# Hybrid diffusion block on one core: paired value products in the array's columns, norms by tile, latent norms inside the window attention, modulation rows turned by transposes, twelve expert slots in layer 1

## The reference

```python
mod = silu(c) @ ada_w + ada_b                       # 6 x 1024, for latent and for context
h = modulate(rms_norm(x, norm1), mod[0], mod[1])
z = h @ w_in                                        # one projection, 15 parts
oa = neighbourhood_attention(...)                   # 4 heads of 64, keys: window + 256 context
q, k, v = mla_heads(rms_norm(dq), rms_norm(dkv), kr)   # latent norms, rotary part
ob = block_attention(q, k, v)                       # 4 heads, 96-wide scores, 64-wide values
oc = gated_linear_attention(...)                    # two directions, chunks of 64
y = (sigmoid(m_a)*(oa @ w_br_a) + sigmoid(m_b)*(ob @ w_br_b) + sigmoid(m_c)*(oc @ w_br_c)) @ w_out
x = x + mod[2] * y
x = x + mod[5] * expert_choice_moe(modulate(rms_norm(x, norm2), mod[3], mod[4]))   # 16 experts, 1024 x 1024 x 3
```

## Time and profile before

| | us |
|---|---|
| median of 3 runs | 2928.09 |
| the profiled execution's own time | 2929.94 |
| its span | 2928.2 |
| TensorE busy (matmul) | 2626.2 |
| VectorE busy | 1042.5 |
| ScalarE busy | 689.8 |
| GpSimd busy | 73.1 |

### The profile page before, as it was taken

One profiled execution on the slowest core, in us unless ns is written; L12 is line 12 of the kernel. 1 busy time (PEld: TensorE's weight loads), 2 busy tenths in 40 slices (PEclk: granted clock), 3 DMA queues, 4 the chain that ended last, 5 costly groups with the idle time before them and its releaser, 6 DMA issues.

```text
span 2928.2 us, 42639 instructions
## 1 busy us (share of the span) xinstructions
PE 2626.2 (90%) x17806; PEld 1726.6 (59%) x17806; DVE 1042.5 (36%) x2187; ACT 689.8 (24%) x1330; POOL 73.1 (2%) x131
## 2 busy tenths in 40 slices
PE   5999999899997699999999689999899768999996
PEld 3888877677775535453454478787677642433332
DVE  3534344333672412212221563444347421111112
ACT  2521122322441212121121262133235210110101
POOL 1000100000000000000000000000000000000000
PEclk7999999999998699999999799999899879999998
DMA  5110465155532088786979211132115329999995
GB/s 196 51 44 30 122 195 173 51 166 168 201 136 115 11 329 349 290 347 259 378 283 364 97 36 59 44 101 69 62 51 180 152 91 409 382 407 378 410 386 232
DMA packets 239139, 571.27 MB, mean 195 GB/s; under 512 B 11079, under 2 KB 119857, under 8 KB 237937
## 3 DMA queue, kind: packets, MB, share of 16 engines
q1 hardware_dynamic: 231200, 547.07, 50.4%
q0 software_dynamic: 7760, 21.60, 2.4%
HBM read 548.64 MB, written 19.98 MB: 194 GB/s over the span
## 4 chain that ended last, share of the span: by engine, by line
PE 82%; DVE 8%; DMA 5%; ACT 3%; issue 2%; SPq 0%; DVEq 0%; POOL 0%; ACTq 0%
PE ps L890 12%; PE ps L1305 11%; PE ps L917 11%; PE ps L1435 6%; PE ps L1256 4%; PE ps L1239 4%; PE ps L1149 3%; DMA arena<-in_moe_w_up 3%; PE ps L1454 3%; PE ps L1477 2%; PE ps L1498 2%; PE ps L1328 2%; PE ps L1332 2%; PE ps L859 2%; PE ps L1388 1%
## 5 line engine op out<-in xcount | busy, mean ns | idle before, releaser
L1305 PE MATMUL ps<-arena 128*32 128x512 f32 x2304 | 344.1, 605 | 5.9 <-issue 4.9
L917 PE MATMUL ps<-h_hi,m_lo 128*128 128x512 f32 (+1 forms) x1152 | 345.9, 371 | 1.7 <-DVE arena L1997 1.7
L1306 PE MATMUL ps<-arena 128*32 128x512 f32 x768 | 343.7, 605 | 0.0
L1435 PE MATMUL ps<-arena 128*64 128x512 f32 x1024 | 238.9, 613 | 30.8 <-DMA arena<-in_moe_w_up 27.5
L890 PE MATMUL ps<-m_lo,h_hi 128*128 128x256 f32 (+1 forms) x1248 | 238.6, 293 | 5.5 <-DVE m_lo L1970 3.9
L917 PEld LDWEIGHTS ps<-h_hi,m_lo 128*128 128x128 f32 x1152 | 207.8, 190 | 53.6 <-issue 16.8
L1305 PEld LDWEIGHTS ps<-arena 128*32 128x32 f32 x2304 | 93.7, 112 | 229.4 <-issue 226.8
L890 PEld LDWEIGHTS ps<-m_lo,h_hi 128*128 128x128 f32 x1248 | 198.0, 196 | 17.1 <-issue 12.5
L917 PE MATMUL ps<-h_lo,m_lo 128*128 128x512 f32 (+1 forms) x576 | 204.9, 356 | 0.0
L1435 PEld LDWEIGHTS ps<-arena 128*64 128x64 f32 x1024 | 74.6, 140 | 181.9 <-issue 178.0
L890 PE MATMUL ps<-m_lo,h_lo 128*128 128x256 f32 (+1 forms) x624 | 178.2, 286 | 0.0
(11 more groups left out here) (360 smaller groups left out, 4408.4 us busy)
## 6 DMA issues: line engine op xcount, KB each, us to landing
arena<-in_moe_w_gate SPq DMA_DIRECT2D x128, 1024.0 KB, 6.8
arena<-in_moe_w_up SPq DMA_DIRECT2D x128, 1024.0 KB, 8.5
arena<-in_moe_w_down SPq DMA_DIRECT2D x128, 1024.0 KB, 8.3
ring<-in_w_in SPq DMA_DIRECT2D x42, 1024.0 KB, 5.4
arena<-in_ada_w SPq DMA_DIRECT2D x40, 1024.0 KB, 5.5
mix_spill<-arena POOLq DMA_DIRECT2D x48, 256.0 KB, 2.8
ring<-in_w_out SPq DMA_DIRECT2D x4, 2048.0 KB, 10.2
arena<-in_ada_w SPq DMA_DIRECT2D x3, 2048.0 KB, 21.2
```

What stands on the lines that cost most here:

```text
L917: last = mm(to, w[:, k, cols], h[:, k, seg], start=n == 0 and k == 0, stop=n == 2 and k == KD - 1)
L1305: mm(ps[r][32 * b:32 * b + 32, :], c_xg[:, k, j, 32 * b:32 * b + 32], w, start=k == 0, stop=k == KD - 1)
L1306: last = mm(ps[r][96:128, :], c_xg[:, k, j, 32 * r:32 * r + 32], up[:, kk, 512:1024], start=k == 0, stop=k == KD - 1)
L1435: last = mm(bank[64 * c:64 * c + 64, :], p_xg[:, k, j, :], p_raw[(i + c) % PAIR_SLOTS][:, kk, 512 * half:512 * half + 512], start=k == 0, ...
```

## The change

1. **Values.** The two heads of a pair are done together, at every second iteration: v (128 x 64) is now the weight, the turned probabilities (128 x 128) the moving data, and the two heads write partitions 0 to 63 and 64 to 127 of the bank, interleaved. The result is already turned. The sums come as two more products, ones (128 x 64) with a diagonal of the inverted sums (`inverted`, VectorE), and VectorE multiplies the two. The transposes and copies after the attention are gone; the window attention's result waits in `na_oT` and GpSimd copies it to `oT` once. The latent attention's units now go pair by pair as well.
2. **Modulation rows** are turned by two transposes; VectorE adds the four groups in the copy.
3. **Norms by tile**: square, root, inversion and scaling of a tile stand behind that tile's last addition, with the next tiles' additions between. The second half of the gate rows is made between the output projection's tiles. The chunk and spill transfers at the start of layer 1 are issued tile by tile or earlier, and the small memsets of `scan_keep` and `rpb_pad` stand after the first jobs. The final result is stored by tile.
4. **Latent norms** stand inside the window attention: squares of tile u in unit u (0 to 5), root at 6, scaling of tile u-6 in units 6 to 11.
5. **Expert slots**: 12 in layer 1, the four new ones in `x_sb`, `oT` and free parts of the arena.

The core of the diff:

```diff
+SLOTS_OF = (PAIR_SLOTS, PAIR_SLOTS + 4)
...
-        o_tok = carve(ar, 90, NT, 256)
+        na_oT = carve(ar, 90, 2, TOK)
+        sum_diag = carve(ar, 70, 2, P)
...
-        diag, gated = carve(oTf, 0, 4, P), carve(ar, 24, SEQ)
+        diag, gated = carve(ar, 26, 4, P), carve(ar, 24, SEQ)
...
+        p_raw = [carve(ar, 8 * i, 2, D) for i in range(PAIR_SLOTS)] + [carve(x_flat, 0, 2, D), carve(oTf, 0, 2, D), carve(ar, 74, 2, D), carve(ar, 82, 2, D)]
...
+                    sp.wait_ge(hidT_up, before("hidT_up", l))
                     chunk_load(l, 0)
-                    sp.dma_start(x_spill.rearrange("(t p) d -> p t d", p=P), x_sb[:, CT:NT, :]).then_inc(x_saved, 16)
+                    for t in range(CT, NT):
+                        sp.wait_ge(x_ok, before("x_ok", l) - 2 * (NT - 1 - t))
+                        sp.dma_start(x_spill[(t - CT) * P:(t - CT + 1) * P, :], x_sb[:, t, :]).then_inc(x_saved, 16)
                     chunk_load(l, 1)
...
-                    sp.wait_ge(p_used, before("p_used", l) + g * PER_TURN + (i + 1))
+                    sp.wait_ge(p_used, before("p_used", l) + g * PER_TURN + (i + 1 - SLOTS_OF[l] + PAIR_SLOTS))
                     src = a["moe_w_" + matrix][l, bass.ds(g * GE + j, 1), kp * 256:kp * 256 + 256, :]
-                    sp.dma_start(p_raw[i % PAIR_SLOTS], src.rearrange("e (k p) n -> p (e k) n", p=P)
-                                 ).then_inc(pair_in[i % PAIR_SLOTS], 16)
+                    sp.dma_start(p_raw[i % SLOTS_OF[l]], src.rearrange("e (k p) n -> p (e k) n", p=P)
+                                 ).then_inc(pair_in[i % SLOTS_OF[l]], 16)
...
-            sp.wait_ge(fin_ok, SEQ // P)
-            sp.dma_start(out[0].rearrange("(t p) d -> p t d", p=P), fin).then_inc(stored, 16)
-            sp.wait_ge(stored, 16)
+            for ti in range(SEQ // P):
+                sp.wait_ge(fin_ok, ti + 1)
+                sp.dma_start(out[0][ti * P:(ti + 1) * P, :], fin[:, ti, :]).then_inc(stored, 16)
+            sp.wait_ge(stored, 16 * (SEQ // P))
...
+                    if 2 * i == sum(at[0] == "na" for at in MIX_AT[l]):
+                        pool.wait_ge(o_ok, before("o_ok", 2 * l + 1))
+                        cols = slice(q_tiles(l)[0] * P, TOK)
+                        nc.gpsimd.tensor_copy(oT[:, 0:2, cols], na_oT[:, :, cols]).then_inc(na_moved, 1)
...
-                            last = mm(ada_bank(h)[:, 256 + 2 * c:258 + 2 * c], ada_row[0:ADA_ROWS, tile(c)], col_sum[0:ADA_ROWS, :],
-                                      start=True, stop=True)
+                            last = tr(ada_bank(h)[:, 256 + P * c:256 + P * c + ADA_ROWS], ada_row[0:ADA_ROWS, tile(c)], ident[0:ADA_ROWS, 0:ADA_ROWS])
...
-                        pe.wait_ge(o_ok, before("o_ok", idx) + u)
+                    if u >= 2:
+                        pe.wait_ge(o_ok, before("o_ok", idx) + u // 2)
...
+                def values(p):
+                    t = us[2 * p][1]
                     if t >= CT:
-                        pe.wait_ge(p_act, before("p_act", idx) + lats[u])
-                    pe.wait_ge(p_dve, before("p_dve", idx) + u + 1)
+                        pe.wait_ge(p_act, before("p_act", idx) + lats[2 * p + 1])
+                    pe.wait_ge(p_dve, before("p_dve", idx) + 2 * p + 2)
                     keys = range(NT if t >= CT else CT)
                     for kt in keys:
-                        v = nav[:, kt, 64 * h:64 * h + 64] if i == 0 else mv[:, kt, h, :]
-                        last = mm(ps[5][:, 256:320], probT[:, u % 2, kt, :], v, start=kt == 0, stop=kt == keys[-1])
+                        for e in range(2):
+                            h = us[2 * p + e][0]
+                            v = nav[:, kt, 64 * h:64 * h + 64] if i == 0 else mv[:, kt, h, :]
+                            mm(ps[5][64 * e:64 * e + 64, 256:384], v, probT[:, e, kt, :], start=kt == 0, stop=kt == keys[-1])
+                    pe.wait_ge(sum_ok, before("sum_ok", idx) + 2 * p + 2)
+                    for e in range(2):
+                        last = mm(ps[5][64 * e:64 * e + 64, 384:512], ones[:, 0:64], sum_diag[:, e, :], start=True, stop=True)
...
-                    if u >= 2:
-                        values(u - 2)
+                    if u >= 3 and u % 2:
+                        values(u // 2 - 1)
...
-                for ti, t in enumerate(q_tiles(l)):
-                    if ti >= 2:
-                        pe.wait_ge(oT_ok, before("oT_ok", idx) + ti - 1)
-                    for k in range(2):
-                        last = tr(ps[4 + ti % 2][:, tile(k)], o_tok[:, t, tile(k)], ident)
-                    last.then_inc(oT_up, 1)
-                pe.wait_ge(oT_ok, before("oT_ok", idx) + NQ[l])
+                pe.wait_ge(o_ok, before("o_ok", idx) + n // 2)
...
-                            gate_rows(l, 0)
+                            for n in range(2 * NSEG[l]):
+                                gate_row_product(l, n)
+                        if NQ[l] < q <= NQ[l] + 2 * NSEG[l]:
+                            gate_row_product(l, 2 * NSEG[l] + q - NQ[l] - 1)
...
+            def scattered_rows_squared(l, junk):
+                s = 2 * l + 2
+                for ti in range(NORMS[s]):
+                    act.wait_ge(x_ok, before("x_ok", l + 1) - 2 * (NORMS[s] - ti - 1))
+                    square(s, ti, junk)
+                    if ti:
+                        rooted(s, ti - 1)
+                rooted(s, NORMS[s] - 1)
...
+                if u < NT:
+                    t = u
+                    if t in q_tiles(l):
+                        do(lat_junk[:, t % 2, 0:QR], dqb[:, t, 0:QR], ACT.Square, accum_out=mst[:, 0, 6 + t:7 + t])
+                    last = do(lat_junk[:, t % 2, QR:QR + KVR], dqb[:, t, QR:QR + KVR], ACT.Square, accum_out=mst[:, 0, t:t + 1])
...
+                for ti in range(NQ[l]):
+                    act.wait_ge(y_ok, before("y_ok", l) + NQ[l] + ti + 1)
+                    square(s2, ti, xn2)
+                    if ti:
+                        rooted(s2, ti - 1)
+                    if ti < 2 * NSEG[l]:
+                        gate_copied(2 * NSEG[l] + ti)
...
+            def mean(s, ti):
+                t = NT - NORMS[s] + ti
+                dve.wait_ge(nrm_ss, sum(NORMS[:s]) + ti + 1)
+                v.tensor_scalar(st[:, 8 + t:9 + t], st[:, t:t + 1], 1.0 / D, EPS, ALU.mult, ALU.add).then_inc(nrm_ms, 1)
+            def scaled(s, ti):
+                t = NT - NORMS[s] + ti
+                dve.wait_ge(nrm_root, sum(NORMS[:s]) + ti + 1)
+                link(v.reciprocal(st[:, 24 + t:25 + t], st[:, 16 + t:17 + t]))
+                if s == 2 * DEPTH:
+                    v.scalar_tensor_tensor(fin[:, ti, :], x_sb[:, t, :], st[:, 24 + t:25 + t], fin_row, ALU.mult, ALU.mult).then_inc(fin_ok, 1)
+                else:
+                    v.tensor_scalar((xn2 if s % 2 else xn1)[:, t, :], x_sb[:, t, :], st[:, 24 + t:25 + t], None, ALU.mult).then_inc(xn_ok, 1)
+            def normed_behind(s, ti):
+                if ti >= 1:
+                    mean(s, ti - 1)
+                if ti >= 2:
+                    scaled(s, ti - 2)
+            def normed_last(s):
+                mean(s, NORMS[s] - 1)
+                scaled(s, NORMS[s] - 2)
+                scaled(s, NORMS[s] - 1)
...
-                        v.tensor_copy(modT[h // 24][:, m:m + 2, :], ada_bank(h)[:, 256:260].rearrange("p (a b) -> p a b", b=2)
-                                      ).then_inc(ada_raw, 1)
+                        groups = ada_bank(h)[:, 256:512].rearrange("p (c g s) -> p c s g", c=2, g=ADA_COLS)[:, :, 0:2, :]
+                        v.tensor_reduce(modT[h // 24][:, m:m + 2, :], groups, AX_X, ALU.add).then_inc(ada_raw, 1)
...
+                    dve.wait_ge(s_exp, before("s_exp", idx) + u + 1)
+                    if us[u][1] >= CT:
                         link(v.tensor_tensor(st[:, c + 5:c + 6], st[:, c + 3:c + 4], st[:, c + 4:c + 5], ALU.add))
                         link(v.reciprocal(st[:, c + 6:c + 7], st[:, c + 5:c + 6]))
                     else:
                         link(v.reciprocal(st[:, c + 6:c + 7], st[:, c + 4:c + 5]))
-                    v.tensor_scalar(o_tok[:, t, 64 * h:64 * h + 64], ps[5][:, 256:320], st[:, c + 6:c + 7], None, ALU.mult
-                                    ).then_inc(o_ok, 1)
+                    v.tensor_scalar(sum_diag[:, u % 2, :], ident, st[:, c + 6:c + 7], None, ALU.mult).then_inc(sum_ok, 1)
...
+                def normalise(p):
+                    h, t = us[2 * p]
+                    dve.wait_ge(o_up, before("o_up", idx) + p + 1)
+                    to = na_oT[:, h // 2, tile(t)] if i == 0 else oT[:, 2 + h // 2, tile(t)]
+                    link(v.tensor_copy(to, ps[5][:, 256:384]))
+                    v.tensor_tensor(to, to, ps[5][:, 384:512], ALU.mult).then_inc(o_ok, 1)
...
-                        normalise(u - 2)
+                    if u >= 3 and u % 2:
+                        normalise(u // 2 - 1)
...
```

(21 more changed lines are left out.)

271 lines of the change are left out of this document (122 added, 149 removed).

## The result

The changed kernel takes 2802.62 us (median of 4 runs, 2799.69 to 2804.06) where the kernel before took 2927.12 us beside it (4 runs, 2923.57 to 2928.55): ratio 0.9575, 95% interval 0.9559 to 0.9592. That is faster by 124.5 us. The forecast was 2836 with a range of 2804 to 2868, so it had the sign and most of the mechanisms, 92 us of the gain, and missed its own range by 1.4 us. The span of the profiled execution went from 2928.2 to 2801.7 us.

What follows compares the result with a forecast made beforehand. The prediction took TensorE, busy in 90% of the span, as the bound, and loads in layer 1's experts. Nine gains summed to 91.8 us off 2929.94, 2838.1, less 1.85 for the median: 2836 us, range 2804 to 2868.

Steps and rivals of the forecast that it cites:

- a: Modulation rounds at the start of layer 0: transposes and an earlier first round gain 5 us (3.5 to 6.5).
- b: Step from layer 0 to 1: less work behind the last addition, itself 2.3 us later; gain 7.3 us (6 to 8.5).
- c: Norm 2: by-tile gains of 7.7 and 3.9 us, less 3 us for half of six stalls dropping the clock; about 2.5.
- d: Expert slots in layer 1: four more pieces loaded ahead in a load-bound stage gain 10.7 us (9 to 11.5).
- f1: Attention values: 14 column-half products take 1.87 us a pair instead of 2.56; net gain 17 us (5 to 30).
- f2: Waits at values and context transposes in the attentions, with `o_ok` once per pair: gain 6 us (2 to 9).
- f3: Stretches behind the attentions: latent norms hidden in window attention, turns of `o_tok` gone; gain 28 us (25 to 30).
- g: 40 modulation turns in the attentions: two transposes replace each turn, less 2 us for new waits; gain 6 us (3 to 9).
- R1: Rival on the values: column halves work fully beside each other, 1.64 us a pair, gain 29.4; time 2824, chance 0.12.
- R3: Rival on the values: column halves do not overlap, 4.34 us per pair, values -61; time 2914, chance 0.05.
- R4: Rival on the values: each product waits for the other half's full end, 5.32 us per pair; time 2946, chance 0.02.
- R2: Rival: all six norm 2 stalls drop the clock (-8.8 us), extra slots only move the wait (-10.7); 2856, chance 0.12.

Runs made afterwards that it cites:

- e7_mod_products: The changed kernel with the modulation rows turned by products with the constant again instead of transposes; 2819.72 us (ratio 0.9623).
- e10_no_sums: The changed kernel without the two products of ones with the diagonal of inverted sums in each pair of units; 2796.68 us (ratio 0.9544).
- e8_norm_whole: The changed kernel with norm 1 of layer 0 done for all tiles at once, rounds still turned by transposes; 2806.53 us (ratio 0.9578).
- e4_diag_early: The changed kernel with each diagonal of the second half of the gate rows made one tile earlier on VectorE; 2781.31 us (ratio 0.9492).
- e5_heads_in_turn: The changed kernel with a pair's twelve value products ordered one head after the other instead of by turns; 2835.73 us (ratio 0.9675).

## Why the prediction was wrong, by its own steps

| step | forecast | measured | read from |
|---|---|---|---|
| a, start | 5 | 9.2 | table |
| b, layer 0 to 1 | 7.3 | 9.2 | table |
| c, norm 2 | 2.5 | 4.4 | table |
| d, slots | 10.7 | 24.7 | table; 9.9 head start, some 15 depth |
| e, tail | 9.3 | 10.6 | table |
| f1, values | 17 | 28 | 0.88 us in each of 32 pairs |
| f2, halved waits | 6 | about 2 | rest of the attentions |
| f3, behind the attentions | 28 | 28 | 25.9 (34.0 us from the last values to the next stage before, 8.2 now), and 1.7 in the latent heads |
| g, 40 turns | 6 | 8.7 | e7_mod_products |
| projection stretches, routing | 0 | 2.2 | table |

**The step that failed is d**: "the stage is bound by loads: 4 x 1.0486 / 0.393 = 10.7 us (9 to 11.5)". It priced the four slots by their bytes alone, on a mean rate taken as the rate of the memory. That part came true, 9.9 us; the depth, some 15 us more, was in the sum at nothing. The transfers had a second number in reach, 409 to 410 GB/s in most windows of 12 us of the same stage, and a stage with a DMA share of 1.00 and TensorE busy for 92% is one in which two sides change places; there a ring's depth is worth more than its bytes. The DMA share could not show it: it was still 0.95 at 363 GB/s. With the right 24.7 in the sum, and nothing else changed, the forecast would have been 2822, its error 19 us instead of 33. The bounds of d, 9 to 11.5, held no case of this kind. The range was also narrowed by "Not all terms miss to one side": seven of the nine terms came out above their forecast and only f2 clearly below, and the sum of the high ends, 2802.2, would just have held the result. Two small slips in the sum (all six drops in c make 11.6 - 18 = -6.4, not -7, and 22 - 4.4 in f1 is 17.6, not 17) change nothing here.

**f1 was mis-sized.** "four products ... take 0.59 us (199.71 to 200.30), 0.147 each": this was most likely a burst of four with 0.15 us for the burst in it. 0.59 is just what four products of the new kind take (e10_no_sums, context pairs). I also charged 0.1 us behind each burst a second time. The upper bound, 30, held it. The Trainium skill, "TensorEngine Tiling (Array Packing)", Key Properties, says that a change of the tiling mode drains TensorE and that tiles run side by side; the 0.15 us for a burst and the 1.68 against 2.60 us by turns and in turn agree with both. The old bursts, in full width, have no such fixed part: six products take 1.28 us and two take 0.38 to 0.39, as in

```profile
359.81 0.55 PE L1149 MATMUL ps<-arena 128*128 128x64 f32 x4
360.19 0.56 PE L845 MATMUL ps<-cst,ada_row 98*128 98x2 f32 x4
```

That the 0.15 us is the drain isn't shown, only that it comes with the column halves. The same page's "Up to 2×" (Theoretical Speedup) is met per product: 0.213 before, 0.11 now, and the two additional products and the burst's own 0.15 leave 1.68 against 2.56. Of the loss by the fast weight load, which the forecast had as a second point against this part, no run shows anything. The measured 1.68 us a pair is nearer to R1's 1.64 than to the 1.87 of the forecast. R3 and R4, at 4.34 and 5.32, are refuted.

**a** missed the clock. The forecast priced eight rounds at the low level throughout; e7_mod_products and e8_norm_whole show that with transposes the higher level comes within the rounds (in the changed kernel and in e8_norm_whole in the third one), wherever the rounds start. Of the 9.2 us, 2.3 are the earlier first round (28.91 against 31.20; about 1 was forecast) and 6.9 the transposes (4 was forecast).

**c** held as a mechanism: six waits of 2.1 to 2.2 us, with dropped clocks behind. That its size came out within 2 us is luck in part: five waits dropped the clock and not three, but a drop cost 1.9 us (e4_diag_early) and not the 3 that I took, 9.6 against 9. The 2 us are in the rest, where the gate products between tiles cost less than the 1.1 us that I took: without a drop the next product starts 0.56 us behind. **b** assumed the last addition 2.3 us late; it was 1.0 (655.8 against 654.9 us behind the start of the layer's experts). **e**, **f3** and **g** are right within 3 us; **f2** was hoped for, not read: over the four attentions TensorE's idle time was 24.9 us and is 24.4. The rival R2 failed in its second half (the slots gave more, not nothing). In its first it was near in kind, with five of six drops, and not in price: norm 2 gained 4.4 us instead of losing 6.4.

## What to carry to other kernels

Where a stage shows one side at 1.00 and the other above 90%, look at windows no longer than the ring takes to turn once (here 8 pieces of 2.6 us) before pricing it: if the rate changes, both sides bound it by turns, and one more buffer is worth more than the bytes that it loads ahead. Price a burst as a fixed part and a part per instruction, from two bursts of different length. And where a small wait stands inside dense products of TensorE, make its input one step earlier: here six waits of 2 us cost 21.

## What the runs showed of the hardware

- Column halves on TensorE run beside each other when their products stand close together. Fourteen products of 128 x 64 weights by 128 columns take 1.68 us by turns and 2.60 us with six of the one half ahead of six of the other; six products take 0.81 us by turns and with two and two alike (e5_heads_in_turn). How far apart the partners may stand no run tells.
- The windows view prints a granted clock of 1.00 also where the trace holds no record of the clock. In the trace of e7_mod_products the first record starts at 58.9 us. In the first two lines below the 1.00 therefore says nothing: the rounds take the 2.77 us that they took in the kernel before at a recorded 0.50. The next two are from TensorE's timeline on either side of 58.9 us: the product gets shorter just where the record begins. So ahead of a trace's first record the durations are the evidence.

```profile
34.00:38.00 4.00, 4.00 (x32) 2.17 (x24) 0.69 (x3) 0.78 (x1) 0.00 (x0) 1.00 1.05 383
42.00:46.00 4.00, 3.86 (x29) 1.40 (x22) 3.10 (x4) 0.00 (x0) 0.00 (x0) 1.00 0.00 0
...
56.56 0.63 PE L902 MATMUL ps<-h_lo,m_lo 128*128 128x512 f32 x1
59.36 0.40 PE L902 MATMUL ps<-h_lo,m_lo 128*128 128x512 f32 x1
```

- Why the clock rises in the rounds with transposes and doesn't with products stays open. All ten kernels with transposes show the rise there, the two with products (the kernel before and e7_mod_products) don't.
